# A third buffer for scaled attention scores, in the region of the transposed activations

## The chip, the cores and the metric

The kernel runs as one program on one core of one Trainium2 chip. The metric is the time of one execution on the device in microseconds; with one core, that core's time is the kernel's. The core's engines are TensorE (PE in the profile: matmuls and transposes), VectorE (DVE), ScalarE (ACT), GpSimd (POOL) and SyncE (SP), which here issues nearly all transfers of weights from HBM; 16 DMA engines carry them. The engines run side by side and are ordered by semaphores alone.

## The reference

Two transformer blocks work on 256 tokens of width 1024, all in float32. The first has two layers (a Fourier and convolution mixer, then windowed attention), each followed by a mixture of 16 experts; the second has one layer with mixers of its own and a routed mixture. The change touches the windowed attention of the first block's second layer: 16 query heads of width 64, four of which share one key and value head, and blocks of 128 queries. With 256 tokens each block of queries sees all 256 keys through a mask:

```python
s = jnp.einsum("bnqkgd,bnjkd->bnkgqj", qb, kb) * (HEAD_DIM ** -0.5)
s = jnp.where(valid[None, :, None, None], s, -jnp.inf)
m = jnp.maximum(jnp.max(s, axis=-1, keepdims=True), sink_l)
e = jnp.exp(s - m)
p = e / (jnp.sum(e, axis=-1, keepdims=True) + jnp.exp(sink_l - m))
o = jnp.einsum("bnkgqj,bnjkd->bnqkgd", p, vb).reshape(B, S, qd)
return o @ w_out
```

## The kernel before

**Weights** pass through `ring`, eight slots of 1 MB each. SyncE issues pieces in a fixed order and, ahead of each, waits until TensorE has used the piece that held its slot (`place_free`, semaphore `piece_used`). In the order of the pieces the attention's projection (`P_QKV`) is followed by those of the modulations 9 to 13 (`ada_w`), four for the output projection (`P_ATT_OUT`), two that go beside the ring into `work` for the next block (`w_in_2`), the modulations 15 and 16 and then the experts (`P_MOE_B`). A modulation's four pieces are multiplied with the conditioning vector (`ada_piece`, 8 matmuls of 512 columns); its row is then turned into columns (`as_columns`) and copied by VectorE (`columns_out`, L2701).

**The heads.** The queries of a tile of 128 tokens and the four heads that share a key head make a group; there are 2 tiles x 4 key heads = 8 groups, numbered 0 to 7. A group's scores are 128 x (4 x 256) values. They lie scaled and masked in `sc`, which has two buffers; group g uses buffer g % 2. Every engine has its own loop over the groups, written out by hand, and works on a group in this order:

- TensorE: scores of g into `ps` (banks 0 to 3 by turns in the first tile, banks 0 and 1 in the second).
- VectorE: scale and mask into `sc` (L784, "mask g" below), row maximum (L788), three small operations (L789 to L792), after which `negmax_ready` is raised.
- ScalarE: four exponentials in place, each with its sum, and a small one for the sink (all of ScalarE's work has line L2518, a helper's).
- VectorE: sum and reciprocal (L801, L802), product in place (L803, "product g"), raising `probs_ready`.
- TensorE: eight transposes of `sc` into banks 4 and 5 (L2150, "transposes g"), raising `pT_ps`; then work of its own beside the group (`beside_probs`: pieces of modulation 13 in turns 3 to 5, a unit of the first tile's output projection in turns 5 to 8).
- ScalarE: copy of the transposed scores to `pT`.
- TensorE: the weighted sum with the values, 16 matmuls (L2147 like all matmuls that aren't transposes); ScalarE copies it to `oT`.

The turns are shifted against one another. In turn g TensorE does scores g+1, transposes g-1, the work beside and weighted sum g-1; VectorE does mask g and then product g-1, with `columns_out` between them in turns 3 and 7; ScalarE does exponentials g, then the copies of g-1. Scores g wait (`masked`) until the banks they go to have been read: by mask g-2 up to g = 4, by mask g-1 above. Mask g, from g = 2 on, waits for `pT_ps` to reach g-1, that is for transposes g-2, which are the last to read its buffer of `sc`.

**The region of the change.** `hT`, eight rows of 256 values on each of 128 partitions, holds the transposed activations. The projection to queries, keys and values is its last reader before the heads; the entry to the experts (L2784) writes it next.

After the loop TensorE does the gate's rows and the second tile's output projection (`out_unit(1, kp)`, four pieces, 32 matmuls), each of which gives back its slot of the ring, then modulation 15 and the entry to the experts.

Of the kernel before, what the change touches and what calls it, by code (L numbers as in the profile page):

```python
# [26 lines left out]
ACT = mybir.ActivationFunctionType  # L27
X = mybir.AxisListType.X

P = 128  # L30
# [15 lines left out]
REP = NH // NKV  # L46
# [141 lines left out]
def build(nc, A, WHERE):  # L188

    with ExitStack() as ctx:  # L190
        def sb(name, shape, dt=F32):
            return ctx.enter_context(nc.sbuf_tensor(name, shape, dt))
# [3 lines left out]
        def S(name):  # L196

            if name not in sems:
                sems[name] = ctx.enter_context(nc.semaphore(name))
            return sems[name]  # L200

        def then(eng, ins, name):

            made[name] = made.get(name, 0) + 1
            ins.then_inc(S(name), 1)
            eng.wait_ge(S(name), made[name])
# [11 lines left out]
        ps = ctx.enter_context(nc.psum_tensor("ps", [P, 8, 512], F32))  # L218
# [3 lines left out]
        hT = sb("hT", [P, KD, SEQ])  # L222
# [141 lines left out]
        def copied(g):  # L364

            return turned(g) - 1
# [53 lines left out]
        sc = attention_area(2, REP, SEQ)  # L420
# [97 lines left out]
        place = moe2_area(NT, E)  # L518
# [34 lines left out]
        NG = NT * NKV  # L553
        ADA_13_IN_GROUP = {3: range(1), 4: range(1, 3), 5: range(3, 4)}

        def scores_bank(g):

            return 2 * (g % 2) if g < NKV else 0

        def pe_attention(pe, mm, tr, h_ready, gate_row, ada_piece, ada_block, as_columns):  # L560
# [37 lines left out]
            def scores(g):  # L598
                _, T, kv = groups[g]
                if g == 0:  # L600
                    pe.wait_ge(S("kT_ready"), NT)
                if g < 2:
                    pe.wait_ge(S("qT_ready"), g + 1)
                else:

                    pe.wait_ge(S("masked"), g - 1 if g <= NKV else g)
                for a_ in range(2):
                    for b in range(2):
                        o = slice(HD * b, HD * b + HD)
                        last = mm(ps[:, scores_bank(g) + b, SEQ * a_:SEQ * a_ + SEQ],  # L610
                                  qT[o, 2 * kv + a_, P * T:P * T + P], kT2[o, kv, :], a_ == 0, True)
                last.then_inc(S("scores_ps"), 1)
# [31 lines left out]
            for g in range(NG + 1):  # L644
                if g + 1 < NG:
                    scores(g + 1)
                if g == 0:
                    ada_block(11)
                    pe.wait_ge(S("mod_copied"), copied(9))
                    ada_block(12)  # L650
                    pe.wait_ge(S("row_copied"), read(11))
                    pe.wait_ge(S("mod_copied"), copied(10))
                if g:
                    g1, T, kv = groups[g - 1]
                    pe.wait_ge(S("probs_ready"), g1 + 1)
                    for place in range(REP):
                        for kt in range(NT):
                            last = tr(ps[:, 4 + place // 2, SEQ * (place % 2) + P * kt:SEQ * (place % 2) + P * kt + P],
                                      sc[:, g1 % 2, place, P * kt:P * kt + P])
                    last.then_inc(S("pT_ps"), 1)  # L660
                    beside_probs(g)
                    pe.wait_ge(S("pT_ready"), g1 + 1)
                    if g1 >= 2:
                        pe.wait_ge(S("oT_ready"), g1 - 1)
                    for a_ in range(2):
                        for b in range(2):
                            for kt in range(NT):
                                last = mm(ps[HD * b:HD * b + HD, 6, SEQ * (g1 % 2) + P * a_:SEQ * (g1 % 2) + P * a_ + P],
                                          vs[:, kt, HD * kv:HD * kv + HD], pT[:, 2 * b + a_, kt, :],
                                          a_ == 0 and kt == 0, kt == NT - 1)  # L670
                    last.then_inc(S("oT_ps"), 1)
                if g == 6:
                    as_columns(13)
# [7 lines left out]
        def act_attention(sc_, act_, ada_rows):  # L681
            ada_rows(8)
            sc_.wait_ge(S("aside_arg"), 6)
            act_(trig, ang[:, 0:2], ACT.Sin).then_inc(S("aside_done"), 1)
            ada_rows(9)
            for T in range(NT):
                sc_.wait_ge(S("kT_ps"), T + 1)
                act_(kT2[:, :, P * T:P * T + P], ps[:, 4 + T, :].rearrange("p (k s) -> p k s", k=NKV), ACT.Copy)\
                    .then_inc(S("kT_ready"), 1)
            ada_rows(10)  # L690
            for T in range(NT):
                sc_.wait_ge(S("qT_ps"), T + 1)
                act_(qT[:, :, P * T:P * T + P], ps[:, 2 * T:2 * T + 2, :].rearrange("p b (j s) -> p (b j) s", j=4),
                     ACT.Copy).then_inc(S("qT_ready"), 1)
            groups = head_groups()
            for g in range(NG + 1):
                if g < NG:
                    st = sm_[:, g % 2]
                    sc_.wait_ge(S("negmax_ready"), g + 1)
                    for place in range(REP):  # L700
                        act_(sc[:, g % 2, place], sc[:, g % 2, place], ACT.Exp, bias=st[:, place:place + 1],
                             accum_out=st[:, 4 + place:5 + place])
                    act_(st[:, 8:12], st[:, 8:12], ACT.Exp).then_inc(S("exps_ready"), 1)
                if g < 2:
                    ada_rows(11 + g)
                if g:
                    g1, T, kv = groups[g - 1]
                    sc_.wait_ge(S("pT_ps"), g1 + 1)
                    if g1:
                        sc_.wait_ge(S("oT_ps"), g1)  # L710
                    act_(pT.rearrange("p h k s -> p (h k s)"), ps[:, 4:6, :].rearrange("p b s -> p (b s)"), ACT.Copy)\
                        .then_inc(S("pT_ready"), 1)
                    sc_.wait_ge(S("oT_ps"), g1 + 1)
                    act_(oT[:, 2 * kv:2 * kv + 2, P * T:P * T + P],
                         ps[:, 6, SEQ * (g1 % 2):SEQ * (g1 % 2) + SEQ].rearrange("p (a s) -> p a s", a=2), ACT.Copy)\
                        .then_inc(S("oT_ready"), 1)
                if g == 5:
                    ada_rows(13)
# [14 lines left out]
        def dve_attention(dve, v, link, gate_sum, update_x, bias_and_gains, router, columns_out):  # L733
# [42 lines left out]
            for g in range(NG + 1):  # L776
                if g < NG:
                    _, T, kv = groups[g]
                    st = sm_[:, g % 2]
                    dve.wait_ge(S("scores_ps"), g + 1)  # L780
                    if g >= 2:

                        dve.wait_ge(S("pT_ps"), g - 1)
                    then(dve, v.scalar_tensor_tensor(  # L784
                        sc[:, g % 2], ps[:, scores_bank(g):scores_bank(g) + 2, :]
                        .rearrange("p b (a s) -> p (b a) s", a=2), HD ** -0.5, window[:, T].unsqueeze(1).broadcast_to([P, REP, SEQ]),
                        op0=ALU.mult, op1=ALU.add), "masked")
                    link(v.reduce_max(st[:, 0:4], sc[:, g % 2], X))  # L788
                    link(v.tensor_tensor(st[:, 0:4].rearrange("p (b a) -> p b a", a=2),  # L789
                                         st[:, 0:4].rearrange("p (b a) -> p b a", a=2), sink[:, kv], ALU.max))  # L790
                    link(v.tensor_scalar(st[:, 0:4], st[:, 0:4], -1.0, None, ALU.mult))
                    then(dve, v.tensor_tensor(st[:, 8:12].rearrange("p (b a) -> p b a", a=2),  # L792
                                              st[:, 0:4].rearrange("p (b a) -> p b a", a=2), sink[:, kv], ALU.add),
                         "negmax_ready")
                if g in (3, 7):
                    columns_out(12 if g == 3 else 13)
                if g:
                    g1 = g - 1
                    st = sm_[:, g1 % 2]
                    dve.wait_ge(S("exps_ready"), g1 + 1)  # L800
                    link(v.tensor_tensor(st[:, 4:8], st[:, 4:8], st[:, 8:12], ALU.add))  # L801
                    link(v.reciprocal(st[:, 4:8], st[:, 4:8]))  # L802
                    then(dve, v.tensor_tensor(sc[:, g1 % 2], sc[:, g1 % 2],  # L803
                                              st[:, 4:8].unsqueeze(2).broadcast_to([P, REP, SEQ]), ALU.mult),
                         "probs_ready")

# [2268 lines left out]
```

## Time and profile before

| what | value |
|---|---|
| median of 3 runs | 1763.52 us (1758.71 to 1771.0) |
| profiled execution | 1758.08 us, its span 1756.3 us |
| mean granted TensorE clock | 0.898 |
| TensorE busy | 1355.8 us (77%) |
| VectorE busy | 439.8 us (25%) |
| ScalarE busy | 223.2 us (13%) |
| HBM read | 637.40 MB, 364 GB/s over the span |
| loop over the heads | first mask 696.3 us, last weighted sum to 761.8 us |

A row of instructions reads: start, duration, engine, line, operation, output <- input tiles, shapes and count; in brackets the time for which the engine was idle before it and what ended that. `sc`, `qT`, `pT` and others are parts of the tile `work`, and are shown by that name. A row of a stretch reads: stretch, length, busy time of the engines with the number of instructions, granted clock as a share of full speed, share of the DMA engines' time, GB/s. Several instructions of one kind in a row are merged to one row with a count.

### The profile page before, as it was taken

The page shows a single profiled execution, that of the slowest core. Times are in us where ns is not written, and L with a number is a line of the kernel's source. Part 1 is how long each engine was busy: PE and PEld are TensorE (multiplying, and loading weights), DVE is VectorE, ACT ScalarE, POOL GpSimd, SP SyncE. Part 2 cuts the span into 40 slices and gives each one's busy share as a digit, 9 for nine tenths or more (in the row PEclk, how much of TensorE's full clock was granted, in tenths as well). Part 3 has the DMA queues.
Part 4 walks back from the last instruction along what each step waited for, and adds up shares of the span by engine and source line. Part 5 has one row for each costly group of instructions (what it writes and reads, how often), then busy time and mean ns, then how long its engine had stood idle before and what let it go on. Part 6 is the DMA issues. An engine that isn't in the chain of part 4 may idle for free.

```text
span 1756.3 us, 25665 instructions
## 1 busy us (share of the span) xinstructions
PE 1355.8 (77%) x11264; PEld 736.3 (42%) x11264; DVE 439.8 (25%) x1014; ACT 223.2 (13%) x470; POOL 25.7 (1%) x46
## 2 busy tenths in 40 slices
PE   7999665666666579897766666655699888999997
PEld 4755332332323234553323333322346645655553
DVE  1674211013100024643101000000126465322122
ACT  2122000000000021531000000000112233100001
POOL 1000000000000000000000000000020000000000
PEclk9998888888888899998788787788899999999999
DMA  9999999999999997849999999999951325899996
GB/s 375 362 367 358 427 423 427 423 426 424 426 424 426 424 407 299 343 170 399 424 425 424 426 424 427 423 426 424 419 208 65 144 109 195 345 421 421 421 420 256
DMA packets 89484, 640.11 MB, mean 364 GB/s; under 512 B 8508, under 2 KB 8508, under 8 KB 43296
## 3 DMA queue, kind: packets, MB, share of 16 engines
q1 hardware_dynamic: 85712, 625.85, 86.8%
q0 software_dynamic: 3664, 12.64, 2.0%
q8 instruction: 90, 1.47, 0.3%
q14 instruction: 18, 0.15, 0.0%
HBM read 637.40 MB, written 1.96 MB: 364 GB/s over the span
## 4 chain that ended last, share of the span: by engine, by line
DMA 48%; PE 44%; DVE 5%; ACT 1%; issue 1%; SPq 0%; DVEq 0%; ACTq 0%
PE ps L2147 42%; DMA ring<-in_moe_w_up 31%; DMA ring<-in_moe_w_down 13%; PE ps L2150 2%; DMA ring<-in_fc_w_in 2%; DMA ring<-in_attn_w_qkv 1%; DMA ring<-in_moe_w 1%; DMA ring<-in_ada_w 1%; ACT work L2518 1%; DVE work L803 0%; SPq L322 0%; DVE work L2923 0%; DVE work L784 0%; DVE work L788 0%; ACT hT L2518 0%
## 5 line engine op out<-in xcount | busy, mean ns | idle before, releaser
L2147 PE MATMUL ps<-ring,work 128*32 128x256 f32 (+3 forms) x7696 | 754.7, 457 | 330.1 <-DMA ring<-in_moe_w_gate 151.1
L2147 PEld LDWEIGHTS ps<-ring,work 128*32 128x32 f32 (+2 forms) x7696 | 349.4, 131 | 714.9 <-issue 268.7
L2518 ACT ACTIVATE work<-ps 128x256 f32<-128x256 f32 (+3 forms) x171 | 79.0, 467 | 1213.9 <-PE ps L2147 1019.3
L2957 DVE TENSOR_TENSOR work<-work,ps 128x256 f32<-128x256 f32 x32 | 13.5, 421 | 622.3 <-ACT work L2518 622.3
L2147 PE MATMUL ps<-work 32*128 32x256 f32 (+7 forms) x1098 | 155.5, 447 | 10.0 <-ACT work L2518 6.6
L2147 PEld LDWEIGHTS ps<-work 32*128 32x128 f32 (+4 forms) x1098 | 89.2, 199 | 73.7 <-issue 58.5
L2147 PE MATMUL ps<-ring,hT 128*128 128x512 f32 (+1 forms) x224 | 92.3, 573 | 6.1 <-DMA ring<-in_attn_w_qkv 3.0
L2150 PE MATMUL ps<-const,work 128*128 128x128 f32 (+1 forms) x392 | 64.0, 294 | 13.2 <-DVE work L803 6.1
L2147 PE MATMUL ps<-ring,condT 128*32 128x512 f32 x560 | 71.4, 630 | 3.0 <-DMA ring<-in_ada_w 3.0
L2147 PE MATMUL ps<-hT,ring 128*128 128x256 f32 x288 | 67.4, 395 | 4.2 <-DMA ring<-in_fc_w_in 2.6
L2147 PE MATMUL ps<-work,xn 128*128 128x128 f32 (+2 forms) x448 | 66.6, 300 | 1.8 <-DVE work L1905 1.6
L2150 PEld LDWEIGHTS ps<-const,work 128*128 128x128 f32 (+1 forms) x392 | 46.6, 161 | 48.2 <-issue 23.1
L2147 PEld LDWEIGHTS ps<-ring,hT 128*128 128x128 f32 x224 | 43.3, 195 | 54.8 <-issue 49.4
L2147 PEld LDWEIGHTS ps<-hT,ring 128*128 128x128 f32 x288 | 56.4, 198 | 16.1 <-issue 4.7
L2147 PEld LDWEIGHTS ps<-work,xn 128*128 128x128 f32 x448 | 58.1, 191 | 9.2 <-issue 7.0
L2975 DVE TENSOR_TENSOR work<-ps,gate 128x256 f32<-128x256 f32 x32 | 13.6, 425 | 153.4 <-PE ps L2147 153.4
L2850 DVE SCALAR_TENSOR_TENSOR work<-work,cols 128x256 f32<-128x256 f32 x120 | 47.6, 477 | 0.0
L2518 ACT ACT_TABLE_LOAD x28 | 35.9, 1283 | 1.8 <-DVE condT L2706 1.4
L2147 PEld LDWEIGHTS ps<-ring,condT 128*32 128x32 f32 x560 | 16.9, 115 | 43.4 <-issue 36.2
L2518 ACT ACTIVATE work<-work 128x256 f32<-128x256 f32 (+7 forms) x55 | 27.4, 500 | 47.5 <-DVE work L1735 14.5
L1967 DVE TENSOR_TENSOR work<-work,ps 128x256 f32<-128x256 f32 x17 | 7.2, 421 | 92.2 <-PE ps L2147 92.1
L2942 DVE TENSOR_SCALAR work<-ps,gain,mod 128x128 f32<-128x128 f32 x56 | 19.1, 404 | 28.1 <-PE ps L2147 28.0
(305 smaller groups left out, 655.2 us busy)
## 6 DMA issues: line engine op xcount, KB each, us to landing
ring<-in_moe_w_up SPq DMA_DIRECT2D x64, 2048.0 KB, 17.8
ring<-in_moe_w_down SPq DMA_DIRECT2D x128, 1024.0 KB, 15.9
ring<-in_moe_w_gate SPq DMA_DIRECT2D x63, 2048.0 KB, 16.9
ring<-in_moe_w SPq DMA_DIRECT2D x102, 1024.0 KB, 10.9
ring<-in_ada_w SPq DMA_DIRECT2D x70, 1024.0 KB, 10.4
ring<-in_w_in SPq DMA_DIRECT2D x10, 1024.0 KB, 18.1
ring<-in_fc_w_in SPq DMA_DIRECT2D x6, 1024.0 KB, 15.8
ring<-in_attn_w_qkv SPq DMA_DIRECT2D x6, 1024.0 KB, 20.3
```

What stands on the lines that cost most here:

```text
L1967: v.tensor_tensor(hid3, act3, ps[:, 5, 0:SEQ], ALU.mult).then_inc(S("hid3_ready"), 1)
L2147: return pe.matmul(out, lhsT, rhs, start=start, stop=stop, skip_group_check=True)
L2150: return pe.matmul(out, in_, ident[0:n, 0:n], is_transpose=True, start=True, stop=True, skip_group_check=True)
L2518: return nc.scalar.activation(out, in_, f, **kw)
L2850: ins = v.scalar_tensor_tensor(cv[:, g, :], src, w, cv[:, g, :], op0=ALU.mult, op1=ALU.add)
L2942: v.tensor_scalar(xe[:, c % 2, j, :], ps[:, bank, P * (j % 4):P * (j % 4) + P], gain[:, site, j:j + 1], mod[:, 3 * site, j % 4, j // 4, 0: ...
L2957: v.tensor_tensor(hid, act, ps[:, 5, 0:SEQ], ALU.mult).then_inc(S("hid_ready"), 1)
L2975: v.tensor_tensor(ye, ps[:, 7, 0:SEQ], gate[:, 0:SEQ], ALU.mult).then_inc(S("ye_ready"), 1)
```

## The change

Groups 2 and 5 keep their scaled scores in the first four rows of `hT`; the others use `sc[g % 3]`, which for them is 0 or 1. A group's buffer is thus used again three groups later and not two, and mask g waits, from g = 3 on, for transposes g-3. Masks of groups 0 to 2 have no such wait. The small tile of sums (`sm_`) keeps its two buffers.

```diff
--- before.py
+++ after.py
@@ -553,6 +553,10 @@
         NG = NT * NKV
         ADA_13_IN_GROUP = {3: range(1), 4: range(1, 3), 5: range(3, 4)}
 
+        def score_rows(g):
+
+            return hT[:, 0:REP, :] if g % 3 == 2 else sc[:, g % 3]
+
         def scores_bank(g):
 
             return 2 * (g % 2) if g < NKV else 0
@@ -656,7 +660,7 @@
                     for place in range(REP):
                         for kt in range(NT):
                             last = tr(ps[:, 4 + place // 2, SEQ * (place % 2) + P * kt:SEQ * (place % 2) + P * kt + P],
-                                      sc[:, g1 % 2, place, P * kt:P * kt + P])
+                                      score_rows(g1)[:, place, P * kt:P * kt + P])
                     last.then_inc(S("pT_ps"), 1)
                     beside_probs(g)
                     pe.wait_ge(S("pT_ready"), g1 + 1)
@@ -698,7 +702,7 @@
                     st = sm_[:, g % 2]
                     sc_.wait_ge(S("negmax_ready"), g + 1)
                     for place in range(REP):
-                        act_(sc[:, g % 2, place], sc[:, g % 2, place], ACT.Exp, bias=st[:, place:place + 1],
+                        act_(score_rows(g)[:, place], score_rows(g)[:, place], ACT.Exp, bias=st[:, place:place + 1],
                              accum_out=st[:, 4 + place:5 + place])
                     act_(st[:, 8:12], st[:, 8:12], ACT.Exp).then_inc(S("exps_ready"), 1)
                 if g < 2:
@@ -778,14 +782,14 @@
                     _, T, kv = groups[g]
                     st = sm_[:, g % 2]
                     dve.wait_ge(S("scores_ps"), g + 1)
-                    if g >= 2:
-
-                        dve.wait_ge(S("pT_ps"), g - 1)
+                    if g >= 3:
+
+                        dve.wait_ge(S("pT_ps"), g - 2)
                     then(dve, v.scalar_tensor_tensor(
-                        sc[:, g % 2], ps[:, scores_bank(g):scores_bank(g) + 2, :]
+                        score_rows(g), ps[:, scores_bank(g):scores_bank(g) + 2, :]
                         .rearrange("p b (a s) -> p (b a) s", a=2), HD ** -0.5, window[:, T].unsqueeze(1).broadcast_to([P, REP, SEQ]),
                         op0=ALU.mult, op1=ALU.add), "masked")
-                    link(v.reduce_max(st[:, 0:4], sc[:, g % 2], X))
+                    link(v.reduce_max(st[:, 0:4], score_rows(g), X))
                     link(v.tensor_tensor(st[:, 0:4].rearrange("p (b a) -> p b a", a=2),
                                          st[:, 0:4].rearrange("p (b a) -> p b a", a=2), sink[:, kv], ALU.max))
                     link(v.tensor_scalar(st[:, 0:4], st[:, 0:4], -1.0, None, ALU.mult))
@@ -800,7 +804,7 @@
                     dve.wait_ge(S("exps_ready"), g1 + 1)
                     link(v.tensor_tensor(st[:, 4:8], st[:, 4:8], st[:, 8:12], ALU.add))
                     link(v.reciprocal(st[:, 4:8], st[:, 4:8]))
-                    then(dve, v.tensor_tensor(sc[:, g1 % 2], sc[:, g1 % 2],
+                    then(dve, v.tensor_tensor(score_rows(g1), score_rows(g1),
                                               st[:, 4:8].unsqueeze(2).broadcast_to([P, REP, SEQ]), ALU.mult),
                          "probs_ready")
```

## Rows read from the trace of the kernel before

**Rows 1.** The page: chain that ended last, shares of the span.

```profile
DMA 48%; PE 44%; DVE 5%; ACT 1%; issue 1%; SPq 0%; DVEq 0%; ACTq 0%
```

**Rows 2.** Busy time by stretches: PE, PEld, DVE, ACT, POOL, clock, DMA share, GB/s.

```profile
742.00:767.00 25.00, 22.64 (x106) 12.50 (x106) 9.13 (x21) 8.07 (x20) 0.00 (x0) 0.93 0.00 1
767.00:807.00 40.00, 38.79 (x286) 23.25 (x288) 21.28 (x57) 11.27 (x18) 0.54 (x1) 0.91 0.90 336
807.00:1266.00 459.00, 295.76 (x3412) 141.75 (x3400) 33.84 (x85) 14.94 (x36) 0.00 (x0) 0.82 1.01 424
```

**Rows 3.** Instructions in order of time, transfer queue: start, duration, operation.

```profile
722.81 12.38 SPq L322 DMA_DIRECT2D ring<-in_ada_w  x4
...
767.67 10.67 SPq L322 DMA_DIRECT2D ring<-in_ada_w  x4
```

**Rows 4.** Line of the mask; VectorE's waits; a product in order of time.

```profile
L784 DVE SCALAR_TENSOR_TENSOR work<-ps,work x8: 1224/1225/1226, 696.3 to 741.7; 128x1024 f32<-128x1024 f32 x8
...
DVE work L784 <- PE ps L2150: 13.5, 6, 4.4
...
712.29 1.22 DVE L803 TENSOR_TENSOR work<-work 128x1024 f32<-128x1024 f32 x1
```

**Rows 5.** Order of time, VectorE: the masks of groups 2 and 6.

```profile
708.76 1.23 DVE L784 SCALAR_TENSOR_TENSOR work<-ps,work 128x1024 f32<-128x1024 f32 x1 [4.36 <-PE ps L2150]
...
733.90 1.22 DVE L784 SCALAR_TENSOR_TENSOR work<-ps,work 128x1024 f32<-128x1024 f32 x1 [1.28 <-PE ps L2150]
```

**Rows 6.** Order of time, TensorE: scores 2, sums and scores, transposes 1 to 4.

```profile
706.47 1.13 PE L2147 MATMUL ps<-work 64*128 64x256 f32 x8
707.53 1.09 PE L2150 MATMUL ps<-const,work 128*128 128x128 f32 x8
709.74 2.21 PE L2147 MATMUL ps<-work 128*64 128x128 f32 x24 [1.11 <-ACT work L2518]
713.57 1.09 PE L2150 MATMUL ps<-const,work 128*128 128x128 f32 x8 [1.62 <-DVE work L803]
...
719.74 1.97 PE L2150 MATMUL ps<-const,work 128*128 128x128 f32 x8
...
726.64 1.09 PE L2150 MATMUL ps<-const,work 128*128 128x128 f32 x8 [1.61 <-DVE work L803]
727.67 1.92 PE L2147 MATMUL ps<-ring,condT 128*32 128x512 f32 x16
...
732.67 1.09 PE L2150 MATMUL ps<-const,work 128*128 128x128 f32 x8 [0.94 <-DVE work L803]
```

**Rows 7.** Order of time, ScalarE: output's copy, an exponential, transposed scores' copy.

```profile
710.92 0.38 ACT L2518 ACTIVATE work<-ps 128x256 f32<-128x256 f32 x1 [1.24 <-PE ps L2147]
...
712.38 0.49 ACT L2518 ACTIVATE work<-work 128x256 f32<-128x256 f32 x1
...
714.70 1.02 ACT L2518 ACTIVATE work<-ps 128x1024 f32<-128x1024 f32 x1 [0.65 <-PE ps L2150]
```

**Rows 8.** Busy time by stretches, the loop's second half.

```profile
732.70:747.00 14.30, 14.30 (x88) 8.15 (x88) 7.44 (x13) 6.20 (x20) 0.00 (x0) 1.00 0.53 212
```

**Rows 9.** Order of time, VectorE and TensorE: after modulation 13's columns.

```profile
747.16 0.18 DVE L2701 COPY mod<-ps 128x24 f32<-128x24 f32 x1 [2.39 <-PE ps L2147]
...
748.94 1.88 PE L2150 MATMUL ps<-const,work 128*128 128x128 f32 x8 [1.89 <-DVE work L803]
```

**Rows 10.** Order of time, VectorE: a pass of other tiles.

```profile
779.31 1.23 DVE L2823 TENSOR_TENSOR x<-x,tmp 128x1024 f32<-128x1024 f32 x1
```

**Rows 11.** Busy time by stretches, around the two falls of the clock.

```profile
711.70:715.10 3.40, 1.78 (x18) 1.54 (x14) 2.01 (x5) 2.58 (x10) 0.00 (x0) 0.98 1.02 407
715.10:721.90 6.80, 6.80 (x40) 5.17 (x43) 4.34 (x10) 3.21 (x12) 0.00 (x0) 0.51 1.03 410
745.80:749.20 3.40, 1.51 (x15) 1.26 (x12) 1.90 (x6) 2.44 (x10) 0.00 (x0) 0.98 0.00 0
749.20:752.60 3.40, 3.40 (x11) 2.37 (x10) 2.08 (x6) 1.02 (x1) 0.00 (x0) 0.52 0.00 0
```

## The prediction

> **What bounds the kernel now.** The page's chain that ended last comes first: it lies 48% in weight transfers and 44% on TensorE [rows 1], so an edit to VectorE's order matters only where VectorE stands in that chain. The table by stretches comes next. From 807 to 1266 us the DMA engines are full at 424 GB/s: expert weights bind. From 742 to 767 they move nothing while TensorE is busy 22.64 of 25 us; from 767 to 807 they fill again [rows 2]. The transfer queue says why they stop: four 1 MB pieces go out from 722.81 to 735.19, the next at 767.67, when the output projection of the second tile has given back its first slot [rows 3]. So the heads' loop holds up both TensorE and the weight stream, and a microsecond saved in it starts both earlier. Third, the waits: VectorE's mask (L784) waited six times for transposes (L2150), 13.5 us in all, on an engine whose mask and product take 1.22 to 1.23 us each [rows 4]. Last, the rows in order of time. Mask 6 starts at 733.90, 1.28 us after VectorE fell idle; transposes 3 and 4, at 726.64 and 732.67, show the period where nothing disturbs, 6.03 us [rows 5, 6]. In it the mask of group g waits for the transposes of g-2, those for the product (L803) of g-2, and that product stands behind mask g-1 on VectorE: a ring of VectorE work, 4.75 us (mask 2 at 708.76 to the end of the product at 713.51) [rows 4, 5], and 1.28 us of transposes and hand-overs.
>
> **The change, part by part.**
> *The wait.* Six masks (g = 2 to 7) lose the wait for the transposes two groups back. Masks 3 to 7 wait instead for those three groups back, which TensorE has finished before the product of g-2 is even used: nothing. No instruction, DMA or other wait is added or moved, and what queues behind each mask on VectorE is the same as before. What counts is what is late next.
> Mask 2: its scores, 706.47 to 707.60. Masks start 0.14 us after what they wait for (transposes 0, whose place is between these scores and the copy, end at 708.62, mask 2 starts at 708.76), so it comes at 707.74, 1.02 us earlier [rows 5, 6]. They can't come sooner, being behind the modulation's matmuls on TensorE. Transposes 1 then follow at 713.57 - 1.02 = 712.55. Mask 3 finds its scores ready: they are the last eight of the 24 matmuls that end at 711.95, before VectorE is free.
> The period after that: VectorE alone needs 4.75 us. ScalarE's ring is the copy of the transposed scores, 1.02, the weighted sum on TensorE with hand-overs, 1.2 (to 710.92 from the copy's end, which is the transposes' end at 708.62 and 0.06 + 1.02 more), the copy of the output, 0.38, and the exponentials: four at 0.49 us from start to start and a small one of 0.19, 2.15, with a gap or two of 0.04; 4.8 us [rows 7]. The two are level, and I take 4.85 for what their hand-overs cost each other. Transposes 3 come at 712.55 + 2 x 4.85 = 722.25 instead of 726.64, 4.4 us earlier. Of this, 0.87 us is a disturbance that was there before (719.74 to 726.64 is 6.90, not 6.03), treated under the clock.
> From there TensorE binds. Between transposes 3 and 4 it must do the transposes (1.03 to the next start), two pieces of modulation 13 (1.92), weighted sum and scores (2.21, as in group 0): 5.16 us where 6.03 were spent [rows 6]. Transposes 4 start at 727.4, not 732.67: **5.3 us earlier**.
> *The second half gives nothing more.* From 732.7 to 747.0 TensorE is busy without a gap [rows 8]: from here each group has an output-projection unit beside it. Then the columns of modulation 13 leave TensorE, VectorE, which has waited 2.39 us for them in L2701, goes on to product 6, and transposes 6 start at 748.94 after a wait of 1.89 [rows 9]. Mask 7 loses its wait, but stands before L2701 on VectorE, where the earlier mask only waits longer. All this keeps its distance to transposes 4. Cost 0; the cover is TensorE's work, and if it were gone, the mask's wait (under 2.5 us in this group) would count.
> *The place of the third buffer.* Groups 2 and 5 use hT. The nearest row for another tile is a product of x and tmp of the same size, 1.23 us against 1.22 of L803 [rows 4, 10]: between 0 and 0.01 us for each of twelve passes. I take 0. Masks now run beside TensorE's transposes. Mask 2 already ran beside ScalarE's copy of transposed scores, released by the same event, and all eight masks took 1224 to 1226 ns: 0 again.
> *Weights in time.* The output projection's pieces are needed 5 us earlier, at about 729. Behind them in the queue went two pieces of the next block's weights and four of modulation 15, 6.3 MB, all in before 742. At 424 GB/s these take 15 us, so the projection's pieces were in by 727. 0, bound 1 us.
> *After the loop.* TensorE's work from 762 to 807 and the issue at 767.67 are released step by step by the loop's end; all of it shifts.
> Sum 5.3 us. The profiled execution took 1758.08 us (span 1756.3 and 1.8 around it), so 1752.8 by its own measure. The timed runs were 1758.7, 1763.5 and 1771.0. The middle of the four is (1758.7 + 1763.5)/2 = 1761.1, and less 5.3 a median should be **1756 us**.
> *The clock.* TensorE's granted clock falls to 1.2 GHz twice: from 715.1 for 6.8 us (mean 0.51) and from 749.2 for 3.4 us (0.52). In the 3.4 us ahead of each it was busy 1.78 and 1.51 us [rows 11]. The change fills the first gap, since transposes 1 come 1.0 us sooner and the next 2.2; it leaves the second, the columns' round trip. So the sum has the first fall gone and keeps the second. If the first stays, it costs at most half its length, 3.4 us, and the gain is 1.9. The second costs half of 3.4, 1.7.
> The Trainium skill, "TensorE: Matmul & The Clock Gate", section "What's actually happening", has the throttled clock as the default, which activity lifts. The trace agrees as to the order of gap and fall. By that rule a denser loop is the safer one.
>
> **The rivals.**
> *Both falls vanish.* The second gap stays as long but lies 5.3 us earlier and may fall differently. Gain 5.3 + 1.7 = 7.0: 1754. For: the stretch ahead of it was hardly idler than the one ahead of the first. Against: the gap remains. Chance 0.2.
> *The first fall stays.* Gain 1.9: 1759. Chance 0.1.
> *The wait only changes its name, or the stream hides it.* If scores held up mask 3 and later ones too, or the experts' transfers did not hang on the loop, the gain would be 0 to 1: 1760 to 1761. Against: scores 3 end at 711.95, and 25 us without a byte. Chance 0.1.
> *Slower.* The fall of the clock moves from where there was slack into TensorE's bound part, from transposes 4 to the modulation behind the output projection (727 to 782). Half clock costs half its length there, so it decides from 10.6 us on. Two more stretches like the first, 6.8 us each, cost 6.8: net 1.5 slower, 1762.6. For: falls come after gaps, and the columns' gap stands right before this part's long run. Against: from 742 to 767 the mean clock was 0.93 with that same gap in it [rows 2]. Chance 0.07.
> The forecast itself has 0.53, with a gain of 4.3 to 6.3.
>
> **How the numbers follow.** Low end: the profiled execution less the largest gain, 1758.1 - 7.0 = 1751, taken to 1750 for the hand-overs' estimate. High end: the highest run less the forecast, 1771.0 - 5.3 = 1766. Most of the width is the spread of the executions (12 us), not of the mechanisms. A measurement tells 1%, 17.6 us, from no change. All six waits together are 13.5 us, so no case reaches that: within 1% 0.95, faster 0.03, slower 0.02, both for disturbed runs.
>
> **What would show it.** L784's idle time behind L2150 falls from 13.5 us to under 1, and its first gap, 4.36 us, shrinks to 3.3 and ends with scores. Masks start near 707.7, 712.5, 717.4, 722.3, 727.5 and 735; transposes have a period of 4.8 to 5.2 up to the fourth. The clock stays at 2.4 GHz from 714 to 723. The issue at 767.67 comes near 762.4, the experts end 5 us earlier with the stream still at 424 GB/s, and the span is shorter by as much. I am wrong if transposes 4 start later than 729, if the issue moves but the experts' end doesn't, or if L784, L788 or L803 take longer on groups 2 and 5.

## The result and the profile after

The changed kernel takes 1752.07 us in the median of 20 runs (1748.65 to 1762.83), the kernel before 1761.62 in the median of 20. The ratio of their runs is 0.9962, with a 95% interval from 0.9945 to 0.9978: 6.7 us less, between 3.9 and 9.7. That is faster, by less than 1%. The forecast was 5.3 us and 1756 us. The profiled execution has a span of 1746.9 us, 9.4 less than the one of before.

Of the page, two lines, as in the table and [rows 1] of before:

```profile
span 1746.9 us, 25665 instructions
...
DMA 48%; PE 45%; DVE 5%; ACT 1%; issue 1%; SPq 0%; DVEq 0%; ACTq 0%
```

The balance of the kernel is the same. The mask now has line 788, the product 807, transposes 2154, TensorE's other matmuls 2151. The mask by its line, and what VectorE waited for in the stretch of the attention (answers to [rows 4]):

```profile
L788 DVE SCALAR_TENSOR_TENSOR work<-ps,work x6: 1224/1224/1225, 694.8 to 733.6; 128x1024 f32<-128x1024 f32 x6
L788 DVE SCALAR_TENSOR_TENSOR hT<-ps,work x2: 1224/1224/1224, 706.2 to 720.6; 128x1024 f32<-128x1024 f32 x2
...
DVE work L788 <- PE ps L2151: 4.0, 4, 3.0
DVE mod L2705 <- PE ps L2151: 3.4, 1, 3.4
DVE hT L788 <- PE ps L2151: 3.3, 1, 3.3
```

No mask waits for transposes any more. Before, VectorE stood idle ahead of its masks for 13.5 us until transposes and 0.5 until scores; now it is 7.3 us, all of it until scores. So about half of the idle time has only changed its name, most of it at masks 2 and 7 (3.32 and 3.04 us). The two masks written to hT take as long as the six others. In order of time, mask 2 and the copy of modulation 13's columns:

```profile
706.20 1.22 DVE L788 SCALAR_TENSOR_TENSOR hT<-ps,work 128x1024 f32<-128x1024 f32 x1 [3.32 <-PE ps L2151]
...
740.16 0.18 DVE L2705 COPY mod<-ps 128x24 f32<-128x24 f32 x1 [3.44 <-PE ps L2151]
```

The copy waits 1.05 us longer than before (3.44 for 2.39): mask 7 now starts 0.17 us after the start of transposes 5 and no longer 1.23, and VectorE then stands at the copy for as much longer.

TensorE in order of time (answers to [rows 6]), from scores 2 to transposes 5:

```profile
704.95 1.13 PE L2151 MATMUL ps<-work 64*128 64x256 f32 x8
706.01 1.09 PE L2154 MATMUL ps<-const,work 128*128 128x128 f32 x8
708.22 2.21 PE L2151 MATMUL ps<-work 128*64 128x128 f32 x24 [1.11 <-ACT work L2522]
711.00 1.09 PE L2154 MATMUL ps<-const,work 128*128 128x128 f32 x8 [0.57 <-DVE work L807]
...
715.87 1.09 PE L2154 MATMUL ps<-const,hT 128*128 128x128 f32 x8 [0.46 <-DVE hT L807]
...
720.66 1.09 PE L2154 MATMUL ps<-const,work 128*128 128x128 f32 x8 [0.37 <-DVE work L807]
721.68 1.92 PE L2151 MATMUL ps<-ring,condT 128*32 128x512 f32 x16
723.53 2.21 PE L2151 MATMUL ps<-work 128*64 128x128 f32 x24
725.67 1.09 PE L2154 MATMUL ps<-const,work 128*128 128x128 f32 x8
...
733.46 1.09 PE L2154 MATMUL ps<-const,hT 128*128 128x128 f32 x8
```

Read the distances between the starts of the transposes: 4.99, 4.87, 4.79, 5.01 us, where the kernel before had 6.04, 6.17, 6.90, 6.03. The gap behind the product has shrunk from 1.6 us to 0.4 to 0.6, and before transposes 4 there is none: there TensorE is the engine that sets the pace (it binds). From transposes 0 to transposes 4 it is 19.66 us against 25.14, **5.48 us less**.

Where the span's 9.4 us are, going by four events in both traces (transposes 0, the gate's rows behind the loop, the end of the experts' weights, the end): 1.5 us lie ahead of transposes 0 (706.01 for 707.53), where the two kernels do the same. 5.8 lie in the loop up to the gate's rows (48.92 for 54.70). 0.5 lie from there to the experts' end (505.5 for 506.0). The remaining 1.6 lie behind it, where again the two do the same; there TensorE's first 48 matmuls alone took 15.08 us in the execution of the changed kernel and 18.23 in that of before. So 5.8 of 9.4 are in the part that was changed, and single executions differ by several microseconds elsewhere.

The stretches around the second gap and the stream, with the columns of [rows 2] and [rows 11]:

```profile
705.00:740.00 35.00, 32.05 (x259) 20.12 (x256) 25.57 (x46) 20.09 (x62) 0.00 (x0) 1.00 0.99 390
...
740.00:742.00 2.00, 0.11 (x2) 0.07 (x2) 1.74 (x5) 1.54 (x7) 0.00 (x0) 0.85 0.00 0
742.00:745.40 3.40, 3.40 (x11) 2.54 (x12) 2.24 (x7) 1.02 (x1) 0.00 (x0) 0.59 0.00 0
...
800.00:1258.00 458.00, 299.85 (x3404) 144.06 (x3396) 33.85 (x85) 14.97 (x36) 0.00 (x0) 0.80 1.01 425
```

The clock is at 2.4 GHz through the loop up to 740; the fall from 715.1 is gone, the second one is there. From the two shares 0.85 and 0.59 it lies at 741.4 to 744.8, so that it begins 0.5 us before transposes 6 start. The stream runs at 425 GB/s as before. The transfer queue's first issue behind the output projection:

```profile
760.38 10.67 SPq L322 DMA_DIRECT2D ring<-in_ada_w  x4
```

That is 7.29 us earlier than in [rows 3], as much as the gate's rows (754.93 for 762.23): 1.5 from ahead of transposes 0, 5.5 up to transposes 4, 0.3 from there.

### The profile page after: what moved, and what is told of

Its sections match the earlier page's. It is cut to its first block, busy times and chain, and to the rows that moved or that the text cites. A ratio compares the mean times of both kernels' runs of the same rounds, so it can differ in the third digit from the quotient of the medians.

```text
span 1746.9 us, 25665 instructions
## 1 busy us (share of the span) xinstructions
PE 1365.3 (78%) x11264; PEld 738.3 (42%) x11264; DVE 439.8 (25%) x1014; ACT 223.0 (13%) x470; POOL 25.7 (1%) x46
## 4 chain that ended last, share of the span: by engine, by line
DMA 48%; PE 45%; DVE 5%; ACT 1%; issue 1%; SPq 0%; DVEq 0%; ACTq 0%
PE ps L2151 43%; DMA ring<-in_moe_w_up 30%; DMA ring<-in_moe_w_down 13%; PE ps L2154 2%; DMA ring<-in_ada_w 2%; DMA ring<-in_fc_w_in 2%; DMA ring<-in_moe_w 1%; ACT work L2522 1%; ACT hT L2522 0%; SPq L322 0%; DVE work L807 0%; DVE work L792 0%; DVE xn L1899 0%; DVE work L1719 0%; DVE x L2821 0%
## 5 line engine op out<-in xcount | busy, mean ns | idle before, releaser
L2151 PE MATMUL ps<-ring,work 128*32 128x256 f32 (+3 forms) x7696 | 764.1, 465 | 319.3 <-DMA ring<-in_moe_w_gate 141.2
L2961 DVE TENSOR_TENSOR work<-work,ps 128x256 f32<-128x256 f32 x32 | 13.5, 421 | 623.4 <-ACT work L2522 623.4
L2151 PE MATMUL ps<-work 32*128 32x256 f32 (+7 forms) x1098 | 149.6, 440 | 9.8 <-ACT work L2522 7.0
L2151 PE MATMUL ps<-ring,condT 128*32 128x512 f32 x560 | 75.6, 657 | 2.9 <-DMA ring<-in_ada_w 2.9
L2151 PE MATMUL ps<-work,xn 128*128 128x128 f32 (+2 forms) x448 | 70.5, 312 | 1.2 <-DVE work L1909 1.0
L2151 PEld LDWEIGHTS ps<-work,xn 128*128 128x128 f32 x448 | 62.0, 203 | 9.4 <-issue 7.1
L2522 ACT ACTIVATE work<-work 128x256 f32<-128x256 f32 (+7 forms) x47 | 23.4, 501 | 42.7 <-DVE work L1739 14.4
```

The lines of the kernel that those rows point to most:

```text
L2151: return pe.matmul(out, lhsT, rhs, start=start, stop=stop, skip_group_check=True)
L2522: return nc.scalar.activation(out, in_, f, **kw)
L2961: v.tensor_tensor(hid, act, ps[:, 5, 0:SEQ], ALU.mult).then_inc(S("hid_ready"), 1)
```

## The experiments

From each kernel's trace I took three lengths: A, from transposes 0 to transposes 4; B, from there to the gate's rows behind the loop; C, from there to the start of TensorE's 48 matmuls at the end of the experts. The falls are those stretches of the granted clock at 1.2 GHz that lie in A and B. Four of the kernels (waits 6 and 7 kept, both in hT, and the two with a short product) were executed once each: of these only the trace is read, since a single time can't tell a few microseconds.

| kernel | buffers | A us | B us | C us | falls in A; in B, us |
|---|---|---|---|---|---|
| before | 2 | 25.14 | 29.56 | 506.0 | 6.8; 3.4 |
| changed | 3 | 19.66 | 29.26 | 505.5 | none; 3.4 |
| changed, once more | 3 | 19.66 | 29.28 | 506.1 | none; 3.4 |
| wait kept | 2 | 24.20 | 27.88 | 506.1 | 3.4; none |
| four buffers | 4 | 19.65 | 30.84 | 506.7 | none; 6.8 |
| waits 6 and 7 kept | 3 | 19.65 | 29.35 | 506.0 | none; 3.4 |
| columns last | 3 | 19.65 | 25.83 | 506.1 | none; none |
| columns last, once more | 3 | 19.65 | 25.82 | 504.4 | none; none |
| both in hT | 2 | 24.22 | 29.56 | 505.8 | none; 3.4 |
| before, columns last | 2 | 25.13 | 25.83 | 506.4 | 6.8; none |
| short product | 3 | 18.52 | 28.76 | 506.2 | none; 3.4 |
| before, short product | 2 | 21.01 | 27.07 | 505.6 | none; none |

**The wait kept.** Is it the wait, or the place of the buffer? The kernel keeps groups 2 and 5 in hT and waits as before, so it works with two buffers in effect:

```diff
-                    if g >= 3:
+                    if g >= 2:
 
-                        dve.wait_ge(S("pT_ps"), g - 2)
+                        dve.wait_ge(S("pT_ps"), g - 1)
```

> The changed kernel with the old wait: groups 2 and 5 keep their scores in hT, but mask g waits for transposes g-2 again. Theory (the removed wait is the whole gain): transposes 4 come 26.6 us after transposes 0 less what a fall of the clock adds or takes, i.e. 24.3 to 25.2 us as before (25.14), not 19.66 as after; VectorE's idle time at the mask behind transposes is 11 to 13.5 us again, and the time is that of the kernel before, ratio 1.000 to it. Rival (the place or the order of buffers gives the gain, e.g. by less contention): 20 us between transposes 0 and 4, and the time of the changed kernel, ratio 0.996.

Ratio to the kernel before 1.000 (0.9976 to 1.0025). A is 24.20 us, the period 6.03 again. (The first figure of the expectation, 26.6, was a slip; the range behind it, 24.3 to 25.2, misses the measured value by 0.1.) Within the loop the removed wait is the whole gain. This run shows two things more. Its clock fell for 3.4 us in A at a cost of next to nothing: A without any fall is 24.22 ("both in hT", below). And in B it did not fall, though TensorE's gap ahead of transposes 6 was there.

**Four buffers.** Does a third one suffice?

```diff
-            return hT[:, 0:REP, :] if g % 3 == 2 else sc[:, g % 3]
+            return hT[:, REP * (g % 4 - 2):REP * (g % 4 - 1), :] if g % 4 >= 2 else sc[:, g % 4]
...
-                    if g >= 3:
+                    if g >= 4:
 
-                        dve.wait_ge(S("pT_ps"), g - 2)
+                        dve.wait_ge(S("pT_ps"), g - 3)
```

> Four buffers (two in sc, two in the eight rows of hT), mask g waits for transposes g-4. Theory (after three buffers the mask is never late by its buffer: VectorE's own 4.78 us per group binds up to transposes 3, TensorE from there): nothing moves, transposes 0 to 4 take 19.66 us within 0.1, the loop the same within 0.2 us unless the clock falls elsewhere. Rival (a third buffer still binds somewhere): transposes 0 to 4 under 19.4 us, some 0.3 to 1 us less per group.

A is 19.65 us: nothing. The ratio to before is 0.9953 (0.9932 to 0.9974), which holds the changed kernel's 0.9962. B is 1.6 us longer, with a fall of 6.8 us where the changed kernel has one of 3.4: the case the expectation excepted.

**Waits 6 and 7 kept.** Which of the six waits were worth something?

```diff
-                        dve.wait_ge(S("pT_ps"), g - 2)
+                        dve.wait_ge(S("pT_ps"), g - 2 if g < 6 else g - 1)
```

> The changed kernel, but masks 6 and 7 wait for transposes two groups back as before. Theory (TensorE binds from transposes 3 on, so the gain comes from masks 2 to 5 alone): transposes 0 to 4 take 19.66 us. For mask 6 the wait would end at transposes 4's start, 0.9 to 1.1 us after its scores; product 5 and transposes 5 lie behind 4.7 us of TensorE's work and do not notice, so transposes 4 to the gate's rows (29.26 us after) stay within 0.2 us but for the clock, and the span has the full gain. Rival (each of the six waits is worth its share, 5.5/6 = 0.9 us): the loop is 1.8 us longer than after.

VectorE's waits in the stretch of the attention:

```profile
DVE work L788 <- PE ps L2154: 4.6, 2, 3.0
DVE hT L788 <- PE ps L2151: 3.3, 1, 3.3
DVE mod L2705 <- PE ps L2151: 2.4, 1, 2.4
DVE work L788 <- PE ps L2151: 0.5, 2, 0.3
```

Two masks wait 4.6 us in all for transposes; the same two had 4.3 of the 13.5 us before. The loop is 49.00 us long, against 48.92, and up to transposes 6 not even these 0.1 us are there: from transposes 0 it is 35.92 us here and 35.93 in the changed kernel (706.01 to 741.94).

```profile
708.25 1.09 PE L2154 MATMUL ps<-const,work 128*128 128x128 f32 x8
...
744.17 1.97 PE L2154 MATMUL ps<-const,work 128*128 128x128 f32 x8 [1.89 <-DVE work L807]
```

The rest lies in the fall of the clock behind (next experiment). So these two waits are worth nothing. The copy waits 2.4 us again, and not 3.4: the later mask 7 only shortens the wait of the copy behind it.

**Columns last.** The gap ahead of transposes 6, and the fall behind it:

```diff
-                if g in (3, 7):
-                    columns_out(12 if g == 3 else 13)
+                if g == 3:
+                    columns_out(12)
...
                         "probs_ready")
+                if g == NG:
+                    columns_out(13)
```

> The changed kernel with VectorE's copy of modulation 13's columns moved behind the last product, out of turn 7. Theory (the second gap, 1.89 us before transposes 6, is VectorE standing in that copy for columns that TensorE makes only just before it wants product 6, and the fall of the clock that follows, 1.97-1.09 and 4.15-3.60 us, comes from the gap): transposes 6 follow the columns' matmuls at once, the gap is under 0.2 us, the clock stays at 2.4 GHz behind it; from transposes 5 (733.46 after) to the gate's rows it takes 21.47 - 1.9 - 1.4 = 18.2 us, the kernel is 3.3 us faster than the changed one, ratio to before 0.994 to 0.995. Rival 1 (the fall of the clock is not tied to that gap and comes anyway): 1.9 us only. Rival 2 (product 6 is late by another wait, ScalarE's exponentials or the mask's scores): gap over 1 us, gain under 1 us.

TensorE in order of time, from modulation 13's columns to transposes 7:

```profile
742.19 1.06 PE L2153 MATMUL ps<-const,mod_row 128*128 128x6 f32 x8
743.11 1.07 PE L2156 MATMUL ps<-const,work 128*128 128x128 f32 x8
744.01 3.60 PE L2153 MATMUL ps<-ring,work 128*128 128x512 f32 x8
747.54 1.14 PE L2153 MATMUL ps<-work 128*64 128x128 f32 x16
748.62 1.09 PE L2156 MATMUL ps<-const,work 128*128 128x128 f32 x8
```

The transposes follow at once, where the changed kernel has this:

```profile
738.99 1.06 PE L2151 MATMUL ps<-const,mod_row 128*128 128x6 f32 x8
741.94 1.97 PE L2154 MATMUL ps<-const,work 128*128 128x128 f32 x8 [1.89 <-DVE work L807]
```

From transposes 5 to the gate's rows it takes 18.04 us and not 21.47: 3.4 less. B without gap and fall is 25.83; with the gap alone 27.88 (the first experiment); so the gap costs 2.05 and a fall of 3.4 us 1.4 (changed) to 1.7 (before).

The difference between 1.4 and 1.7 comes from where the fall begins. It costs half of that part of it in which TensorE works: in the kernel before it begins 0.2 us after transposes 6 start, so TensorE works through all 3.4 us, and it costs 1.68; in the changed kernel 2.8 us of it lie behind the start of transposes 6 and it costs 1.38. With waits 6 and 7 kept these are 3.0 and 1.47, with four buffers 6.0 and 2.96. What lies in the idle gap costs nothing.

The time is 0.9951 of the kernel before's (0.9930 to 0.9971). This interval overlaps the changed kernel's, so both ran once more, beside each other on one chip:

> The changed kernel once more, beside the next one on the same chip. Theory: the loop's transposes 0 to 4 take 19.66 us with no fall of the clock there (0 in 5 loops with a third buffer so far, 3 in 4 with two), transposes 4 to the gate's rows 29.3 us with a fall or 27.9 without; the ratio to before is 0.996 to 0.997. Rival (the first fall's absence was chance): a stretch at 1.2 GHz between transposes 1 and 4 and 20 us or more.

> The changed kernel with VectorE's copy of modulation 13's columns behind the last product, once more. Theory (both edits add up): loop 45.5 us, 2.0 to 3.4 less than the changed kernel; ratio to before 0.995, and 0.998 to 0.999 to the changed one. Rival (what the loop saves is lost behind it): the same time as the changed kernel, though the loop is shorter; then the stretch from the gate's rows to the experts' end is over 508 us.

The changed kernel took 1756.33 us and 0.9978 of before (0.9959 to 0.9997), the one with the columns last 1749.48 and 0.9941 (0.9921 to 0.9962). The changed kernel's ratio was expected at 0.996 to 0.997, which the interval holds. The traces repeat to 0.02 us in A and B. The loop is 45.47 us against 48.94, and C is no longer. This version is faster than the kernel before in both sets of runs. Over all runs the changed kernel has a mean of 1754.7 us (32 runs) and this one of 1751.9 (19), 2.8 us less; with a standard error of 1.2 us that bears the trace's 3.5 us out in sign and rough size only.

**Both in hT.** The kernel before with its two buffers moved to hT, wait unchanged:

```diff
+        def score_rows(g):
+
+            return hT[:, REP * (g % 2):REP * (g % 2) + REP, :]
```

and this used in place of `sc[:, g % 2]` throughout.

> The kernel before with its two buffers both in hT (rows 0 to 3 and 4 to 7), the wait unchanged: the place alone. Theory (the place costs and gives nothing): masks 1.22 to 1.23 us, exponentials 0.49, eight transposes 1.09 each, transposes 0 to 4 24.1 us where the clock doesn't fall (25.1 where it falls as before), transposes 4 to the gate's rows 27.9 to 29.6. Rival (reads and writes of hT differ): a mask or product more than 0.02 us off 1.23.

The masks by their line:

```profile
L788 DVE SCALAR_TENSOR_TENSOR hT<-ps,work x8: 1224/1225/1225, 695.9 to 741.4; 128x1024 f32<-128x1024 f32 x8
its engine sat idle before it (us, times) until:
  PE ps L2154: 13.5, 6
```

The durations are those of [rows 4] to within 1 ns, the waits for transposes are the same 13.5 us. The place is free. A is 24.22 us without a fall, 0.9 less than before's 25.14 with a fall of 6.8.

**Before, columns last.** The same edit of the columns on two buffers.

> The kernel before (two buffers) with VectorE's copy of modulation 13's columns behind the last product. Theory (the two gaps are separate): transposes 0 to 4 stay at 24.1 to 25.1 us; transposes 4 to the gate's rows fall from 27.88 (clock unfallen) to 25.8 us as in the changed kernel with the same edit (25.83), so 2 us, 3.5 where the fall had come too; ratio to before 0.998 to 0.999. Rival (mask 7's wait takes the copy's place, since it now stands directly before product 6): less than 1 us gained.

B is 25.83 us, A 25.13: both theory's values, the two gaps are separate. The ratio, 0.9986 (0.9966 to 1.0007), has the expected middle and does not exclude zero.

**Short product.** What binds the first half now? VectorE's product is done for one of four heads:

```diff
-                    then(dve, v.tensor_tensor(score_rows(g1), score_rows(g1),
-                                              st[:, 4:8].unsqueeze(2).broadcast_to([P, REP, SEQ]), ALU.mult),
+                    then(dve, v.tensor_tensor(score_rows(g1)[:, 0:1], score_rows(g1)[:, 0:1],
+                                              st[:, 4:5].unsqueeze(2).broadcast_to([P, 1, SEQ]), ALU.mult),
```

> The changed kernel with VectorE's product done for one of the four heads of a group only (the other three stay unnormalised): some 0.85 us less per group on VectorE. Only the loop is to be read. Theory (ScalarE's ring of 4.70 us lies just below VectorE's 4.78, and TensorE's 5.01 binds from transposes 3): the copies of the transposed scores of groups 1 to 3 come at a period of 4.70 us, ScalarE idle only for the weighted sum, and transposes 0 to 4 take 18.5 to 19.3 us instead of 19.66. Rival (VectorE alone binds the first half and nothing lies near): three times 0.85 less, 17.1 us.

A is 18.52 us, 1.1 less than 19.66, where the product went from 1.22 to 0.42 us, 0.80 less per group. ScalarE in order of time, copies of the transposed scores:

```profile
712.79 1.00 ACT L2522 ACTIVATE work<-ps 128x1024 f32<-128x1024 f32 x1
715.03 0.38 ACT L2522 ACTIVATE work<-ps 128x256 f32<-128x256 f32 x1 [1.23 <-PE ps L2151]
...
717.37 1.01 ACT L2522 ACTIVATE work<-ps 128x1024 f32<-128x1024 f32 x1
```

Their period is 4.58 us, and ScalarE's only idle time is that for the weighted sum, 1.23 us. ScalarE's ring (its copy, the weighted sum, its second copy and the exponentials, one after the other) lies 0.2 us under VectorE's 4.78; it is 0.1 shorter than I expected here and 0.2 shorter than in the prediction. A faster VectorE would have bought little more.

**Before, short product.** The same in the kernel before.

> The kernel before with the product done for one of the four heads of a group only (the other three stay unnormalised). Only the loop is to be read. Theory (in the old kernel the ring is VectorE's work plus transposes, 6.03 us): the period between transposes falls by all of the saved 0.85 us to 5.15 to 5.2, transposes 0 to 4 from 24.1 to 20.7 us, still above the changed kernel's 19.66. Rival (the wait for the buffer sits beside another of the same length, such as the scores): period above 5.8.

The transposes start 5.23, 5.32, 5.23 and 5.23 us apart: 0.80 off each period of 6.03, all of what the product lost, and A is 21.01 us, a little over the 20.7 expected since I had put the product's saving at 0.85 where it is 0.80. VectorE's time stood in the old ring in full, next to the transposes.

## Why the prediction was right

*The wait was the bound in the first half, and what came late next.* Right: mask 2 ended its wait with scores, 3.32 us after VectorE fell idle (3.3 forecast). The distances from transposes 0 were 4.99, 9.86, 14.65 and 19.66 us; by the sum 5.02, 9.87, 14.72 and 19.9. Its one estimate, 4.85 us per period for VectorE and ScalarE together, was 4.87 and 4.79: VectorE's own 4.78, plus 0.1 for the copy of modulation 12's columns in one of them. That the 4.85 came out so near is in part luck: it was taken for two level rings that cost each other hand-overs. The prediction had VectorE's ring at 4.75, without the 0.03 us from product to next mask, and ScalarE's at 4.8, and the short product showed ScalarE's at 4.58. They were not level, and ScalarE's did not add anything.

*TensorE binds from transposes 3.* Right, 5.01 against 5.16; I had added durations, and at each of the two changes of kind the next matmuls start 0.07 us before the last has ended. The waits of masks 6 and 7 were worth nothing (experiment on waits 6 and 7).

*The sum.* 5.3 forecast, 5.48 measured from transposes 0 to 4. It is made of 4.56 us that the wait costs at full clock (24.22 less 19.66) and 0.92 us for the fall in before (25.14 less 24.22). So a pair of executions without any fall would differ by 4.6 us only. The runs' ratio, 3.9 to 9.7 us, agrees with both and can't tell them apart.

*The clock.* The fall in A appeared in three of four loops with two buffers (6.8, 3.4, 6.8 us) and in none of six with three or four, not counting the two with the short product, which had none either. That is as forecast, and the loss by it in before was rightly taken at 0.87: without it A is 24.22. With two buffers it cost far less than half its length, since most of it lay in TensorE's slack, and the fall of 3.4 us with the wait kept cost nothing to be seen. The bound of 3.4 us that I gave was for a fall in the changed kernel's first half, where TensorE has 0.4 to 0.6 us of slack per group; none came there, so it stays untested. The second fall came in six of seven loops with the gap of 1.89 us, in one of two with a gap of 1.1 (short product), and in none of the three with the columns last: the gap invites it and does not compel it. Its cost of half its length, 1.7 us, held where TensorE worked through all of it; in the changed kernel it began earlier, and that is the 0.3 us by which B is shorter. The forecast had no term for it.

*The place is free, and the weights were in time.* Right: masks take 1224 to 1225 ns in hT and out of it, and the loop has no wait for the projection's weights.

*The stream does not hide the loop.* Right: C is 505.5 to 506.7 us in eleven of twelve traces, with loops between 45.5 and 54.7 us. What is saved in the loop arrives at the experts' end whole. The rival that had it hidden is excluded. The slower one did not occur: no fall but the one of before lay in TensorE's bound part of the changed kernel.

*The median.* 1752.1 us where 1756 was forecast. The median of before, which I had put at 1761.1 from four executions, came out at 1761.6 in 20. The rest is in the gain, 1761.6 less 1752.1 being 9.5 us by medians and 6.7 by the ratio, against 5.3. No step of the sum accounts for it: the loop gave 5.5 us up to transposes 4 and 5.8 in all in the traces, and when the same kernel was run again its median was 1756.3 and its ratio 0.9978, 3.9 us. The forecast lies between the two measurements. What spreads single executions over some 20 us was not looked for, and stays open.

## What to carry to other kernels

Find the ring, that is the closed chain of steps, each waiting for the one before, that repeats every round; not the longest wait. A buffer that one engine gives back to another is worth, per round, the difference between the ring with the wait and the next longest ring, and only up to the point at which another engine's queue binds: here 1.0 to 1.25 us a round for four rounds, and nothing for the last two waits, though these were a third of the waiting time. When the ring is gone, look for the next place at which the pacing engine stands idle; here an unrelated copy, ordered ahead of an urgent product, was worth almost as much (3.5 us in the trace).

## What the runs showed of the hardware

One gap of TensorE can cost nearly twice its length: 1.89 us idle ahead of transposes 6 cost 2.05 us with the order of work around it, and the stretch at 1.2 GHz that mostly follows another 1.4 to 1.7 (a fall of 6.8 us, 3.0: B 30.84 against 27.88). The same gap went without a fall once with two buffers. In all of these the fall costs half of the time for which TensorE works at 1.2 GHz, 2.8 to 6.0 us of it; where TensorE has slack or stands idle, it cost 0.9 us of 6.8 or nothing. Where the clock does the same, the traces of different kernels repeat to 0.02 us within a loop, while the time of the whole program spreads over 20 us (1750 to 1771); lengths between events of the trace told apart on one execution each what the runs' medians could not.
